# Conformer-convolution taps of a hybrid decoder step: three taps in SBUF behind the input products, GpSimd held meanwhile, and another division of taps over the steps

## What is computed

```python
h = x + 0.5 * rms_norm(swiglu(rms_norm(x, f1_pre), f1_wg, f1_wu, f1_wd), f1_post)
u = rms_norm(h, m_pre)
p_all = u @ w_in
ya, buf_a = conformer_conv(p_all[..., OFF_A:OFF_B], conv_a_buf, a_cw, a_cb, a_lg, a_lb)
yb, s_b = gla_mixer(...)      # gated linear attention
yc, buf_c = short_conv(...)
yd = fox_prompt(q, k, v, logf)      # or fox_decode on the paged keys and values
y = jnp.concatenate([ya, yb, yc, yd], axis=-1) @ w_out
...
def conformer_conv(pa, buf, conv_w, conv_b, ln_g, ln_b):
    val, gate = jnp.split(pa, 2, axis=-1)
    a = val * jax.nn.sigmoid(gate)
    xpad = jnp.concatenate([buf.astype(a.dtype), a], axis=1)
    y = causal_depthwise(xpad, conv_w) + conv_b.astype(a.dtype)
    y = jax.nn.silu(layer_norm(y, ln_g, ln_b))
```

## Time and profile before

| | us |
|---|---|
| median of the runs | 1066.25 |
| the profiled execution | 1065.38 |
| its span in the trace | 1063.6 |
| TensorE busy | 1052.0 |
| VectorE busy | 687.2 |
| ScalarE busy | 570.8 |
| GpSimd busy | 278.4 |

### The profile page before, as it was taken

How to read it: one execution, slowest core, us unless ns; L and a number is a source line. 1 busy time by engine, 2 the same in 40 slices (tenths; PEclk the granted TensorE clock), 3 DMA queues, 4 the chain that set the end, 5 groups by cost and what they waited for, 6 DMA issues and landing times. The chain is left out here.

```text
span 1063.6 us, 24197 instructions
## 1 busy us (share of the span) xinstructions
PE 1052.0 (99%) x8978; PEld 1023.3 (96%) x8978; DVE 687.2 (65%) x1032; ACT 570.8 (54%) x970; POOL 278.4 (26%) x344
## 2 busy tenths in 40 slices
PE   8999999999999999999999999999999999999997
PEld 8999999998999999999999999999989999999997
DVE  5666644599977666654476666446999766666442
ACT  6544454576477644454464444546665765444542
POOL 4222220204505222220142222103054233222202
PEclk9999999999999999999999999999999999999999
DMA  7656567452735665556646556763536456565561
GB/s 278 216 178 185 174 218 243 128 160 88 231 100 182 205 191 178 178 171 187 184 131 200 180 176 189 226 202 121 174 101 210 122 175 217 178 189 174 173 187 45
DMA packets 62882, 187.42 MB, mean 176 GB/s; under 512 B 9162, under 2 KB 18514, under 8 KB 62674
## 3 DMA queue, kind: packets, MB, share of 16 engines
q1 hardware_dynamic: 62802, 186.31, 56.1%
HBM read 182.90 MB, written 3.38 MB: 175 GB/s over the span
## 5 line engine op out<-in xcount | busy, mean ns | idle before, releaser
L318 DVE TENSOR_TENSOR w_lo<-raw,w_hi 128x1024 fp32r<-128x1024 f32 (+1 forms) x316 | 412.3, 1310 | 321.9 <-ACT w_hi L308 321.7
L308 ACT ACTIVATE w_hi<-raw 128x1024 fp32r<-128x1024 f32 x336 | 344.3, 1030 | 239.1 <-PE ub L352 170.7
L350 PE MATMUL ub<-hg_hi,w_hi 128*128 128x264 f32 x976 | 281.2, 288 | 0.7 <-issue 0.7
L351 PE MATMUL ub<-hg_lo,w_hi 128*128 128x264 f32 x976 | 276.6, 283 | 0.0
L352 PE MATMUL ub<-hg_hi,w_lo 128*128 128x264 f32 x976 | 276.3, 283 | 0.0
L350 PE MATMUL ub<-act_hi,w_hi 128*128 128x264 f32 x704 | 200.5, 285 | 0.0
L352 PE MATMUL ub<-act_hi,w_lo 128*128 128x264 f32 x704 | 200.0, 284 | 0.0
L351 PE MATMUL ub<-act_lo,w_hi 128*128 128x264 f32 x704 | 199.1, 283 | 0.0
L350 PE MATMUL quad<-hg_hi,w_hi 128*128 128x264 f32 x696 | 198.6, 285 | 0.0
L351 PE MATMUL quad<-hg_lo,w_hi 128*128 128x264 f32 x696 | 197.2, 283 | 0.0
L352 PE MATMUL quad<-hg_hi,w_lo 128*128 128x264 f32 x696 | 197.1, 283 | 0.0
(11 more groups left out here) (262 smaller groups left out, 1283.6 us busy)
## 6 DMA issues: line engine op xcount, KB each, us to landing
raw<-in_w_gu SPq DMA_DIRECT2D x176, 512.0 KB, 4.0
raw<-in_w_dn SPq DMA_DIRECT2D x64, 512.0 KB, 3.9
raw<-in_w_in SPq DMA_DIRECT2D x44, 512.0 KB, 3.8
raw<-in_w_dn SPq DMA_DIRECT2D x32, 384.0 KB, 3.4
raw<-in_w_out SPq DMA_DIRECT2D x16, 512.0 KB, 3.8
pages<-in_cache_k SPq DMA_DIRECT2D x32, 128.0 KB, 3.4
pages<-in_cache_v SPq DMA_DIRECT2D x32, 128.0 KB, 3.2
con<-in_con SPq DMA_DIRECT2D x1, 1192.0 KB
```

What stands on the lines that cost most here:

```text
L308: eng.activation(w_hi[:, slot, 0:w], raw[:, slot, 0:w], ACT.Copy).then_inc(*sig("hi_ready", reps))
L318: eng.tensor_tensor(w_lo[:, slot, 0:w], raw[:, slot, 0:w], w_hi[:, slot, 0:w].bitcast(F32), ALU.subtract)\
L350: eng.matmul(out, a_hi, x_hi[:, k0 + k, :], start=(first and k == 0), stop=False)
L351: eng.matmul(out, a_hi, x_lo[:, k0 + k, :], start=False, stop=False)
```

## The change

The first three taps (six instructions) are made in step 11, straight behind the two input products. They add up in `ymix` in SBUF instead of in PSUM, and so don't wait for the seventh mask; they wait for `a_in`. Tap 3 reads that sum from SBUF and writes the PSUM bank, from there on all is as before. Step 12 has four taps as before (now 3 to 6), step 13 four instead of six, steps 15 to 18 as many as before, step 19 two instead of three.

GpSimd waits for the sixth early tap before its first half of the layer (unit 14), and for the two decode products of step 18 before the halves of unit 21.

```diff
-TAPS = {12: (0, 4), 13: (4, 10), 15: (10, 16), 16: (16, 22), 17: (22, 26), 18: (26, 28), 19: (28, 31)}
+TAPS = {11: (0, 3), 12: (3, 7), 13: (7, 11), 15: (11, 17), 16: (17, 23), 17: (23, 27), 18: (27, 29), 19: (29, 31)}
+EARLY_TAPS = 3
...
-                        y, x, w = taps_sum[:, c * TP:(c + 1) * TP], a_pad[:, c, t:t + TP], par[:, PAR["acw"] + c * TAPS_A + t:PAR["acw"] + c * TAPS_A + t + 1]
+                        x, w = a_pad[:, c, t:t + TP], par[:, PAR["acw"] + c * TAPS_A + t:PAR["acw"] + c * TAPS_A + t + 1]
+                        early, late = ymix[:, YA + c, 0:TP], taps_sum[:, c * TP:(c + 1) * TP]
                         if t == 0:
-                            after(l, b_msk=7)
-                            dve.tensor_scalar(y, x, w, par[:, PAR["acb"] + c:PAR["acb"] + c + 1], ALU.mult, ALU.add).then_inc(*sig("a_tap"))
+                            after(l, a_in=1)
+                            dve.tensor_scalar(early, x, w, par[:, PAR["acb"] + c:PAR["acb"] + c + 1], ALU.mult, ALU.add).then_inc(*sig("a_tap"))
                         else:
                             after(l, a_tap=k - 1)
-                            out = ymix[:, YA + c, 0:TP] if t == TAPS_A - 1 else y
-                            dve.scalar_tensor_tensor(out, x, w, y, ALU.mult, ALU.add).then_inc(*sig("a_tap"))
+                            if t == EARLY_TAPS:
+                                after(l, b_msk=7)
+                            out = early if t < EARLY_TAPS or t == TAPS_A - 1 else late
+                            dve.scalar_tensor_tensor(out, x, w, early if t <= EARLY_TAPS else late, ALU.mult, ALU.add).then_inc(*sig("a_tap"))
...
                 clear_pads(l)
+                after(l, a_tap=2 * EARLY_TAPS)
                 for n in POOLED:
+                    if n == 21:
+                        after(l, a_dp=2)
                     rest_halves(pool, l, n)
```

## The result

| | before | after |
|---|---|---|
| median, us | 1066.93 | 1070.36 |
| lowest to highest | 1065.76 to 1068.16 | 1066.36 to 1074.54 |
| executions | 20 | 20 |
| profiled execution, us (span) | 1065.38 (1063.6) | 1072.09 (1070.3) |

The ratio of the times is 1.0035 [1.0024, 1.0046]. The forecast, 1066.0 with a range up to 1067.6, is missed on the slow side. The times of the changed kernel also lie wide apart: two near 1066.5, eleven from 1068.9 to 1071.3, seven from 1072.1 to 1074.5. The profiled execution is the fourteenth of the twenty in order of time and shows more loss (6.7 us) than the median (3.4 us).

What follows compares the result with a forecast made beforehand. TensorE, busy 1052.0 of 1063.6 us, bounds the kernel, so only its standstills count: 2 layers x (0.0 at the scores' stall + 0.14 before the output projection) = 0.28 us less, median 1066.0. Range 1064.6 to 1067.6.

Steps and rivals of the forecast that it cites:

- Steps 14 to 17: Mixer behind step 13: VectorE 0.2 us later, taken up by its 0.4 us standstill in step 16; held GpSimd costs nothing.
- The products: Step 11: with GpSimd standing still, a_pad's product takes 0.68 for 1.77, a_dec's about 0.2 for 1.27; 2.3 us gained.
- Six early taps: Step 11: two tensor_scalar at 0.27 and four scalar_tensor_tensor at 0.392, 2.11 us together, spending the products' gain.
- the evacuation of unit 11: VectorE, end of step 11: issued at 250.58, 0.17 us earlier; bounds 0.32 earlier and 0.22 later.
- Tap 3 meets GpSimd: Step 12: tap 3's two instructions read SBUF beside GpSimd's halves and cost 2.0 us in place of 0.8.
- qe: Step 13: this product with two SBUF inputs waits for GpSimd's unit 16 and takes 1.3 us; free before at 0.41.
- the evacuation of unit 13: VectorE, end of step 13: issued at 260.70 instead of 260.49, ending at 261.12, with no reserve left.
- the stall: TensorE's idle time before the past-key scores behind unit 14: keeps its 0.85 us in each layer, worth 0.0 us.
- ScalarE's chain as the holder: Before the scores: gapless ScalarE work from unit 11's evacuation (251.21 to 262.12) sets the stall; unit 13's has 0.26 to spare.
- The hold before unit 21 and the tail: Steps 18 and 19: free decode products and one tap less gain 0.14 of 0.29 us before the output projection, per layer.
- Rival A: Steps 12 and 13: GpSimd's halves miss tap 3's pair or qe; 0.6 us less, 1065.6; chance 0.22.
- Rival B: Step 12: VectorE doesn't get in between two consecutive GpSimd halves at 252.02; 2.3 us more, 1068.6; chance 0.10.

Runs made afterwards that it cites:

- x2_before_late_op: The kernel before plus one 0.4 us tap-like VectorE instruction in step 15 whose result nobody reads; 1068.71 us, ratio 1.0021.
- y1_products_held: The kernel before with GpSimd waiting only for the two input products of step 11, old taps; 1062.98 us, ratio 0.9966.
- y4_fewer_in_13: The kernel before with four taps instead of six in step 13, the two others made up in step 17; 1066.37 us, ratio 0.9996.
- y3_hold_over_pair_and_qe: The changed kernel with the qe product moved right behind tap 3 and GpSimd held until it is done; 1068.5 us, ratio 1.002.
- z2_no_dp_hold: The changed kernel without GpSimd's wait for the decode products before unit 21; 1069.54 us, ratio 1.0033.
- x3_hold_over_pair: The changed kernel with GpSimd held until tap 3's two instructions are done; 1067.68 us, ratio 1.0014.
- x1_after_again: The changed kernel measured once more, nothing edited; 1070.09 us, ratio 1.0027.
- x4_scan_held: The changed kernel with GpSimd also waiting for step 17's scan and dstat addition before unit 20; 1066.98 us, ratio 1.0003.
- z4_products_and_dp_held: The kernel before with GpSimd held over step 11's two input products and, before unit 21, over the decode products; 1062.9 us, ratio 0.9967.
- z1_no_hold: The changed kernel without GpSimd's wait for the sixth early tap; 1073.75 us, ratio 1.0068.
- y2_products_and_scan_held: The kernel before with GpSimd held over step 11's two input products and, before unit 20, over the scan and dstat; 1062.83 us, ratio 0.9963.

## Why the prediction was wrong

**The step that failed** is "Steps 14 to 17: VectorE is 0.2 later, but in step 16 it had stood still 0.4 us for TensorE, which takes this up ... Held cost: nothing." It added up slack. The delay was right (0.24 us at pm); but pm, in step 16, comes before that pause, which lies in front of the evacuation of unit 16 (275.34 in before). Steps 16 and 17 hold three kinds of two-input instructions, the very kind for which the prediction had worked out two meetings in steps 12 and 13, and it didn't set them beside GpSimd's halves. Ten traces show what decides at pm. GpSimd's second half of unit 18 starts 1.1 us before pm and ends 0.1 to 0.2 after it has been issued (in x2_before_late_op it starts 1.5 and ends 0.2 before pm). Those two move together: unit 18 is rounded behind scalings for which ScalarE waits for VectorE's st addition (2.19 us in before), so its halves come later when VectorE does. Unit 19 keeps its own time. If ScalarE has rounded it when pm comes, GpSimd goes on at once and VectorE stands under its next half:

| kernel | unit 19 rounded | pm issued | rounded after pm | pm pair, us |
|---|---|---|---|---|
| y1_products_held | 268.72 | 268.05 | 0.67 | 0.40 |
| y4_fewer_in_13 | 270.07 | 269.55 | 0.52 | 0.44 |
| before | 269.93 | 269.69 | 0.24 | 0.45 |
| y3_hold_over_pair_and_qe | 270.19 | 270.01 | 0.18 | 0.45 |
| after | 271.06 | 271.08 | -0.02 | 1.45 |
| z2_no_dp_hold | 271.03 | 271.06 | -0.03 | 1.46 |
| x3_hold_over_pair | 270.09 | 270.14 | -0.05 | 1.46 |
| x1_after_again | 269.81 | 269.92 | -0.11 | 1.45 |
| x4_scan_held | 270.10 | 270.23 | -0.13 | 1.46 |
| x2_before_late_op | 270.00 | 270.23 | -0.23 | 2.41 |

The last column is the fourth less the third, and the line lies between 0.18, free, and -0.02, met. The kernel before thus escaped by 0.06 to 0.26 us, and 0.24 us of lateness crossed the line. The other eighteen mixers in the fourteen traces fit: layer 0 of the four other kernels has 0.43 to 1.01, layer 1 of all fourteen 0.25 to 1.73, and pm is free in all of them (0.39 to 0.44). The rounding itself waits for a load, here the two rows of ScalarE, before and after:

```profile
268.87 1.06 ACT L308 ACTIVATE w_hi<-raw 128x1024 fp32r<-128x1024 f32 x1 [1.59 <-DMA raw<-in_w_in]
```

```profile
270.00 1.06 ACT L309 ACTIVATE w_hi<-raw 128x1024 fp32r<-128x1024 f32 x1 [1.34 <-DMA raw<-in_w_in]
```

It ends 7.58 to 7.84 us behind the start of the scores in the ten traces (7.72 in before), so a kernel this close to the line can go either way in different executions. The spread of the times fits this: the six kernels with 0.43 or more in layer 0 range over 1.0 us or less each (4 to 6 executions, 11 in y4_fewer_in_13), the eight with less over 2.2 us or more (8 to 32 executions; 8.2 us in the changed kernel). It is argued, not shown, since each kernel has one profile. From pm on it is a chain: 0.24 + 1.0, less the 0.38 pause in front of the evacuation of unit 16, makes the scan about 0.9 late, which in before started 0.85 us ahead of GpSimd's unit 20. That unit starts when TensorE has freed a buffer, so it keeps TensorE's time. The scan lands on it, and the addition behind the scan too.

**Step by step.** (1) The products: 0.68 and 0.18, as forecast. (2) Six early taps: 2.24 us (249.53 to 251.77) for 2.11, the two tensor_scalar at 0.65 instead of 0.54; the evacuation of unit 11 0.06 earlier instead of 0.17, inside the bounds. (3) Tap 3 meets GpSimd: 1.99 for 2.0. (4) qe 1.28 for 1.3; the evacuation of unit 13 0.31 later for 0.21; the stall 0.98 for 0.85, so 0.13 lost where 0.0 was forecast and up to 0.4 allowed. ScalarE's chain as the holder was right, as y4_fewer_in_13 shows. (5) Steps 14 to 17: 0 forecast, 2.46 to 2.49 measured, and 1.2 to 1.3 more where the clock fell. (6) The hold before unit 21 and the tail: 0.14 per layer forecast. The wait of 0.29 us in front of the output projection is gone, and it is gone in z2_no_dp_hold as well, while z4_products_and_dp_held, with that hold and three taps in step 19, still has it (0.27 to 0.30): it belongs to the two taps of step 19, not to the hold. (7) The stretch between the layers has no term in the prediction, and 1.2 us were lost there. Rival A is out, since the pair and qe were both met. Rival B had the sign and two thirds of the size (2.3 of 3.4), but by another mechanism at another place: in steps 12 and 13 VectorE did get in between the halves, as forecast. Its chance of 0.10 priced steps 12 and 13 alone; the same kind of meeting had further places in which to happen, and none of them was in the sum.

**Between the layers.** The 1.2 us between the output projection of layer 0 and the scores of layer 1 belong, but for 0.13 of the scores' stall, to the same kind of meeting, by another cause. VectorE's hg_lo (the low part of the next multiplication's input, made from two SBUF inputs) and GpSimd's sums of squares run side by side at the end of the feed-forward; VectorE, GpSimd, TensorE of the changed kernel:

```profile
737.05 0.49 DVE L1085 SCALAR_TENSOR_TENSOR hg_lo<-resid,par,hg_hi 128x264 fp32r<-128x264 f32 x1
737.60 0.44 DVE L1110 TENSOR_TENSOR mb<-yg,quad 128x264 f32<-128x264 f32 x1
...
738.29 1.06 DVE L1085 SCALAR_TENSOR_TENSOR hg_lo<-resid,par,hg_hi 128x264 fp32r<-128x264 f32 x1
...
736.12 2.93 POOL L1448 TENSOR_TENSOR h_acc<-h_acc,h_sq 128x264 f32<-128x264 f32 x3 [10.41 <-ACT h_sq L807]
...
739.40 0.30 PE L371 MATMUL ub<-hg_hi,w_hi 128*16 128x264 f32 x1 [0.48 <-DVE hg_lo L1085]
```

and of before, where GpSimd is the one that is held up and TensorE doesn't wait:

```profile
733.31 0.48 DVE L1084 SCALAR_TENSOR_TENSOR hg_lo<-resid,par,hg_hi 128x264 fp32r<-128x264 f32 x1
...
731.30 8.19 POOL L1444 TENSOR_TENSOR h_acc<-h_acc,h_sq 128x264 f32<-128x264 f32 x8 [10.42 <-ACT h_sq L806]
```

The code there is the same in both. In all seven traces of kernels with the early taps (after, x1, x3, x4, y3, z1, z2) hg_lo is met at this place, in none of the seven with the old taps. Lateness is not what decides: x2_before_late_op enters the stretch 2.6 us late and loses nothing in it (477.10 us from the output projection to the scores of layer 1, before 477.13), and y3_hold_over_pair_and_qe, which is level with before at the output projection (308.84), loses 1.1. In each of the seven, VectorE starts the instruction behind the second hg_lo 0.54 or 0.55 us after it (737.05 to 737.60 above), in the seven others 0.40 or 0.41. So the third hg_lo is issued when GpSimd's next sum has begun. This loss came with the early taps in every trace, whatever was held; what makes the pause of 0.14 us stays open.

The 1.1 us at the start of the program are not the change's. They come with a granted clock of 0.83 between 10 and 20 us in after, z2 and y2_products_and_scan_held, which has the old taps, and in no other trace. TensorE had stood still for 2.07 to 2.33 us before its first unit in these three, and for 0.69 in before.

## What to carry to other kernels

A delay of VectorE isn't paid back by the next pause if a two-input instruction comes first: set every such instruction between the edit and the next real slack beside the other engine's work, at its new time, and note by how much the old schedule escaped. Holding GpSimd back moves its work as a block onto what comes next, so hold it over as little as possible. Here the wait over two products alone gives 3.6 us; the early taps and the new division, with what they set off, took all of that back and 3.4 us more. Look also at stretches whose code is untouched: 1.2 us of the loss lay between the layers.

## What the runs showed of the hardware

A meeting costs a small instruction as much as a large one: 16 elements took 1.14 to 1.23 us (pm in x2_before_late_op and after) and one element 1.03 to 1.06 (dstat), where 0.2 is free. A scan with two SBUF inputs meets GpSimd too (1.79 for 0.68 in after), and so do tensor_scalar instructions with a single SBUF input when both sides are in SBUF (1.75 for two in z1_no_hold, 0.74 when GpSimd stands still); twelve taps with one input in PSUM took 4.78 to 4.80 in every trace in which they were looked at.

TensorE stood still for 2.34 or 2.35 us before the group norm in four traces. In two of them (after, x1_after_again) the granted clock then fell to the lower of its two levels, 1.2 GHz, in the other two (x2_before_late_op, z2_no_dp_hold) it stayed at 2.4. Engines' busy time by stretches, from 280 to 284 us of the changed kernel (columns: stretch, length; busy us and count of PE, PEld, DVE, ACT, POOL; granted clock of TensorE; DMA share; GB/s):

```profile
280.00:282.00 2.00, 0.18 (x1) 0.21 (x2) 2.00 (x5) 1.37 (x3) 0.58 (x1) 0.84 0.90 277
282.00:284.00 2.00, 2.00 (x6) 1.59 (x7) 2.00 (x7) 0.67 (x2) 0.00 (x0) 0.50 0.94 309
```

and of z2_no_dp_hold, with the same wait:

```profile
280.00:282.00 2.00, 0.20 (x1) 0.23 (x2) 2.00 (x5) 1.39 (x3) 0.56 (x1) 1.00 0.96 305
282.00:284.00 2.00, 2.00 (x15) 1.87 (x15) 2.00 (x7) 1.64 (x4) 1.32 (x2) 1.00 1.01 311
```

Between 282 and 284 us the first ran 6 matmuls at a clock of 0.50, the second 15 at 1.00. By the second table the fall costs 1.2 to 1.3 us net (4.83 less 3.64, 3.79 less 2.46; the trace without it gained 0.23 over that stretch, since the wait of 0.29 at its end is gone). It fell in z1_no_hold as well, after a wait of 3.05 us. What decides whether it falls was not found.
